# Hybrid streaming step on one core: the recurrence's cross-block scores from one packed product, and the attention value products in groups of four steps

## The reference, cut to what matters

```python
def stick_breaking_block(q, k, v, q_pos, k_pos):
    z = einsum('bthd,bshd->bhts', q, k) * (SB_HEAD_DIM ** -0.5)
    mask = k_pos[None, :] < q_pos[:, None]
    log_fail = where(mask, log_sigmoid(-z), 0.0)
    after = cumsum(log_fail, axis=3, reverse=True) - log_fail
    a = where(mask, exp(log_sigmoid(z) + after), 0.0)
    return einsum('bhts,bshd->bthd', a, v)

def step(S, blk):                      # HGRN2, blocks of time, S: key x value state
    b = cumsum(lfb, axis=1)            # lfb: log of the forget gate
    kb = -expm1(lfb)
    q_dec, k_inv = qb * exp(b), kb * exp(-b)
    att = where(tril, einsum('bthc,bshc->bhts', q_dec, k_inv), 0.0)
    o = einsum('bhts,bshv->bthv', att, vb) + einsum('bthc,bhcv->bthv', q_dec, S)
    k_end = kb * exp(b_end - b)
    S_new = exp(b_end[:, 0])[..., None] * S + einsum('bshc,bshv->bhcv', k_end, vb)
    return S_new, o
```

## Time and profile before

| | |
|---|---|
| timed runs | 1099.53, 1097.09, 1099.34 us; median 1099.34 |
| profiled execution | 1096.95 us, span 1095.2 us, mean granted clock 0.996 |
| PE busy | 1069.7 us, 98% of the span |
| DVE, ACT, POOL busy | 651.4, 571.3, 133.8 us |
| one pair (attention and recurrence stage) | about 163.4 us, four of them |

### The profile page before, as it was taken

The page is one execution under the profiler, slowest core; times in us unless marked ns, Lnnn a source line. Parts: engine busy times, 40 slices in busy tenths (PEclk is TensorE's granted clock), DMA queues, the critical chain, the costliest instruction groups (busy, mean ns, idle before and its releaser), DMA issues.

```text
span 1095.2 us, 16749 instructions
## 1 busy us (share of the span) xinstructions
PE 1069.7 (98%) x6324; PEld 981.6 (90%) x6324; DVE 651.4 (59%) x1143; ACT 571.3 (52%) x1264; POOL 133.8 (12%) x145
## 2 busy tenths in 40 slices
PE   8999999999999999999999999999999999999995
PEld 5998779998779998779998779999999999999994
DVE  6677798387797377797377797345412221362117
ACT  5557883367883467883467884444032223252221
POOL 0001112011012011012011012001200100121220
PEclk9999999999999999999999999999999999999998
DMA  8041031132031132041131130143111111111144
GB/s 294 1 142 37 20 128 49 54 97 91 20 134 43 61 102 79 23 136 39 60 113 69 32 135 29 39 154 136 43 39 40 39 39 58 40 40 39 40 192 172
DMA packets 41487, 84.86 MB, mean 77 GB/s; under 512 B 2112, under 2 KB 22208, under 8 KB 41280
## 3 DMA queue, kind: packets, MB, share of 16 engines
q1 hardware_dynamic: 40832, 81.43, 22.3%
q10 hardware_dynamic: 576, 2.36, 0.6%
HBM read 67.27 MB, written 16.52 MB: 77 GB/s over the span
## 4 chain that ended last, share of the span: by engine, by line
PE 78%; ACT 9%; DVE 9%; issue 3%; DMA 1%; ACTq 0%; POOL 0%; DVEq 0%; SPq 0%; POOLq 0%
PE bank L673 50%; PE bank L1017 9%; DVE E L1682 3%; PE bank L810 3%; ACT E L1303 2%; ACT SPH L1315 2%; PE bank L840 2%; ACT E L1298 2%; DVE E L1686 1%; PE bank L796 1%; PE bank L683 1%; PE bank L710 1%; PE bank L914 1%; PE bank L959 1%; PE bank L981 1%
## 5 line engine op out<-in xcount | busy, mean ns | idle before, releaser
L673 PE MATMUL bank<-xh,wh 128*128 128x384 f32 x1296 | 438.8, 339 | 3.1 <-issue 2.9
L673 PE MATMUL bank<-xh,wl 128*128 128x384 f32 x1296 | 439.8, 339 | 0.0
L673 PE MATMUL bank<-xl,wh 128*128 128x384 f32 x1296 | 439.3, 339 | 0.0
L673 PEld LDWEIGHTS bank<-xh,wh 128*128 128x128 f32 x1296 | 243.5, 188 | 11.1 <-issue 9.3
L673 PEld LDWEIGHTS bank<-xh,wl 128*128 128x128 f32 x1296 | 243.6, 188 | 4.5 <-issue 2.0
L673 PEld LDWEIGHTS bank<-xl,wh 128*128 128x128 f32 x1296 | 243.5, 188 | 3.1 <-issue 0.2
L1188 ACT ACTIVATE slot<-bank,ngate 128x384 f32<-128x384 f32 x48 | 27.7, 578 | 178.0 <-PE bank L673 175.3
L1455 DVE CAST wh<-wr 128x1024 fp32r<-128x1024 f32 x64 | 43.7, 683 | 99.2 <-PE bank L673 98.1
L1460 DVE TENSOR_TENSOR wl<-wr,wh 128x1024 fp32r<-128x1024 f32 x64 | 90.8, 1419 | 1.9
L1682 DVE SCALAR_TENSOR_TENSOR E<-E,bank 128x512 f32<-128x512 f32 (+3 forms) x96 | 53.1, 553 | 47.8 <-ACT E L1303 47.6
L1315 ACT ACTIVATE SPH<-E 128x512 fp32r<-128x512 f32 (+2 forms) x80 | 45.4, 567 | 48.6 <-DVE E L1686 35.3
(11 more groups left out here) (229 smaller groups left out, 1672.8 us busy)
## 6 DMA issues: line engine op xcount, KB each, us to landing
wr<-wch SPq DMA_DIRECT2D x64, 512.0 KB, 3.6
KTc<-ckT SPq DMA_DIRECT2D x4, 2048.0 KB, 9.4
Vc<-cv SPq DMA_DIRECT2D x4, 2048.0 KB, 8.4
graw<-gated SPq DMA_DIRECT2D x8, 576.0 KB, 8.8
xres<-xT SPq DMA_DIRECT2D x1, 4608.0 KB, 14.2
yT<-yb SPq DMA_DIRECT2D x6, 576.0 KB, 3.0
xw<-xT SPq DMA_DIRECT2D x4, 768.0 KB, 11.4
okT<-kT ACTq DMA_DIRECT2D x4, 576.0 KB, 3.0
```

Source lines behind the costliest of these rows:

```text
L673: i = nc.tensor.matmul(CH[n % 2][:, 0:WIN], weights[:, k, :], rows[:, k, w * WIN:(w + 1) * WIN], start=(m == 0), stop=(m == 23))
```

## The change

Recurrence: the operands are packed. `KP` holds per chunk four blocks of keys: blocks 0 and 1 scaled to the middle of the chunk, block 2 scaled to its end, block 0 scaled to its end. `QP` holds per chunk the queries of blocks 2 and 3 (from the middle), of block 3 and of block 1 (from their block's start). One product of 128 weight columns against 128 columns gives all three pieces that ACT copies; they lie at other places of the bank. DVE makes the operands in another order, two scalings now after the wait for the cached attention's tiles (whose space `KP` uses), and a memset goes.

Attention: `Aw` has five buffers. The value products stand in iterations 6, 10, 14, 18, 22 and 26, four steps each (n-6 to n-3), instead of two steps in each even iteration from 4 to 26. To make room the four rows `zr` share two tiles, at partitions 0 and 32, and the high and low row of `RT` change places from tile to tile.

```diff
-        zr = [take(f"zr{i}", [P, QW])[0] for i in range(4)]
-        aw_o = off[0] + 4 * QW
-        Aw = [take(f"Aw{i}", [P, QW])[0] for i in range(3)]
+        zrows = [take(f"zrows{i}", [P, QW])[0] for i in range(2)]
+        aw_o = off[0] + 3 * 4 * QW
+        Aw = [take(f"Aw{i}", [P, QW])[0] for i in range(5)]
...
-        KB = place("KB", [P, HB + 2 * BLK])
-        QB = place("QB", [P, HB])
-        Q1 = place("Q1", [P, HB])
+        KP = place("KP", [P, SEQ])
+        QP = place("QP", [P, SEQ])
...
+        def row_at(n):
+            return 32 * (n % 4 // 2)
+
+        def zr(n, cols):
+            return zrows[n % 2][row_at(n):row_at(n) + 1, cols]
+
+        def row_high(n, cols):
+            return RT[STEPS[n][2]][row_at(n):row_at(n) + 1, cols]
+
+        def row_low(n, cols):
+            return RT[STEPS[n][2]][32 - row_at(n):33 - row_at(n), cols]
...
-                    if n >= 4 and n % 2 == 0:
-                        wd, j, _ = STEPS[n - 4]
-                        c0 = first_col(n - 4)
-                        if n == 4:
+                    if n >= 6 and n % 4 == 2:
+
+                        if n == 6:
                             need(pe, s_oc, 3 * p)
                             pe.wait_ge(s_te, 6 * p + 3)
-                        if j == 4 * wd + 3:
-                            need(pe, s_gA, 2 * p + wd)
                         pe.wait_ge(s_a, NS * p + n - 2)
                         if diagonal(n - 3):
                             pe.wait_ge(s_am, DIAGS * p + diagonals_until(n - 3))
-                        for h in range(2):
-                            r = slice(DH * h, DH * h + DH)
-                            nc.tensor.matmul(OB[r, c0:QW], v_nat[:, j * P + DH * h:j * P + DH * h + DH],
-                                             Aw[(n - 4 + h) % 3][:, c0:QW], start=(j == 4 * wd + 3), stop=(j == 0),
-                                             skip_group_check=True).then_inc(s_av, 1)
+                        for m in range(n - 6, n - 2):
+                            wd, j, h = STEPS[m]
+                            c0, r = first_col(m), slice(DH * h, DH * h + DH)
+                            if j == 4 * wd + 3 and h == 0:
+                                need(pe, s_gA, 2 * p + wd)
+                            nc.tensor.matmul(OB[r, c0:QW], v_nat[:, j * P + DH * h:j * P + DH * h + DH], Aw[m % 5][:, c0:QW],
+                                             start=(j == 4 * wd + 3), stop=(j == 0), skip_group_check=True).then_inc(s_av, 1)
...
                             if c < NCH:
-                                h0 = 2 * BLK * c
-                                nc.tensor.matmul(Z[2][:, P:P + 64], lf[:, cols], Q1[:, h0:h0 + 64], start=True, stop=True)
-                                i = nc.tensor.matmul(Z[2][:, P + 64:2 * P], KB[:, h0:h0 + P], QB[:, h0:h0 + 64],
-                                                     start=True, stop=True)
+                                i = nc.tensor.matmul(Z[2][:, P:2 * P], KP[:, cols], QP[:, cols], start=True, stop=True)
                             i.then_inc(s_at, 1)
...
-                        need(act, s_av, t - 2)
-                        if m < 2:
+                        need(act, s_av, t - 4)
+                        if m < 5:
                             need(act, s_hg, 3 * p)
-                        nc.scalar.activation(Aw[m % 3][:, c0:QW], ZB[m % 4][:, c0:QW], ACT.Exp).then_inc(s_a, 1)
+                        nc.scalar.activation(Aw[m % 5][:, c0:QW], ZB[m % 4][:, c0:QW], ACT.Exp).then_inc(s_a, 1)
...
-                                nc.scalar.activation(a[0:32, 32:64], z[0:32, P:P + 32], ACT.Copy)
-                                nc.scalar.activation(a[64:96, 96:128], z[64:96, P + 32:P + 64], ACT.Copy)
-                                nc.scalar.activation(a[0:64, 64:128], z[0:64, P + 64:2 * P], ACT.Copy).then_inc(s_ato, 1)
+                                nc.scalar.activation(a[0:32, 32:64], z[96:128, P + 96:P + 128], ACT.Copy)
+                                nc.scalar.activation(a[64:96, 96:128], z[64:96, P + 64:P + 96], ACT.Copy)
+                                nc.scalar.activation(a[0:64, 64:128], z[0:64, P:P + 64], ACT.Copy).then_inc(s_ato, 1)
...
-                for r in (0, 2):
-                    i = V.tensor_tensor(blocks(lf)[:, :, r, :], k[:, :, r, :],
...
-                scale(lambda r: blocks(KB, 2)[:, :, r, :], lambda r: k[:, :, r, :], F_HK, 4, 0, 2)
-                V.memset(KB[:, HB:], 0.0).then_inc(s_hke, 1)
+                for r, at in ((2, 2), (0, 3)):
+                    i = V.tensor_tensor(blocks(KP)[:, :, at, :], k[:, :, r, :],
...
+                scale(lambda r: blocks(KP)[:, :, r, :], lambda r: k[:, :, r, :], F_HK, 4, 0, 2).then_inc(s_hke, 1)
```

More of the change, by code:

```diff
@@ L49 @@
 NCH = SEQ // P
-HB = NCH * 2 * BLK
 F_END, F_HK, F_HQ, F_K, F_Q, F_ALL, F_START, F_W = 0, 40, 72, 104, 120, 136, 144, 160
@@ L1300, in _ @@
                             need(act, s_Sl, SUMS * p + (sums_until(n - 4) if n >= 4 else 0))
-                            nc.scalar.activation(zr[n % 4][0:1, row_col(n):QW], ZB[n % 4][0:1, row_col(n):QW], ACT.Copy)
+                            nc.scalar.activation(zr(n, slice(row_col(n), QW)), ZB[n % 4][0:1, row_col(n):QW], ACT.Copy)
                         act.wait_ge(s_E, t + 1)
@@ L1319, in _ @@
                         act.wait_ge(s_S, SUMS * p + sums_until(m))
-                        nc.scalar.activation(RT[STEPS[m][2]][0:1, cols], zr[m % 4][0:1, cols], ACT.Copy).then_inc(s_Sh, 1)
+                        nc.scalar.activation(row_high(m, cols), zr(m, cols), ACT.Copy).then_inc(s_Sh, 1)
                     recurrence_aside(p, n)
@@ L1519, in later_row @@
                 cols = slice(row_col(m), QW)
-                row = zr[m % 4][0:1, cols]
+                row = zr(m, cols)
                 dve.wait_ge(s_a, NS * p + m + 1)
@@ L1524, in later_row_low @@
             def later_row_low(p, m):
-                h, cols = STEPS[m][2], slice(row_col(m), QW)
+                cols = slice(row_col(m), QW)
                 dve.wait_ge(s_Sh, SUMS * p + sums_until(m))
-                V.tensor_tensor(RT[h][32:33, cols], zr[m % 4][0:1, cols], RT[h][0:1, cols].bitcast(F32),
-                                ALU.subtract).then_inc(s_Sl, 1)
+                V.tensor_tensor(row_low(m, cols), zr(m, cols), row_high(m, cols).bitcast(F32), ALU.subtract).then_inc(s_Sl, 1)
             def values_low(p):
@@ L1588, in chunk_operands @@
                 dve.wait_ge(s_as, 2 * (p + 1))
-                scale(lambda r: blocks(KB, 2)[:, :, r, :], lambda r: k[:, :, r, :], F_HK, 4, 0, 2)
-                V.memset(KB[:, HB:], 0.0).then_inc(s_hke, 1)
+                for r, at in ((2, 2), (0, 3)):
+                    i = V.tensor_tensor(blocks(KP)[:, :, at, :], k[:, :, r, :],
+                                        fac[:, F_END:F_END + NBLK].rearrange("c (n r) -> c n r", r=4)[:, :, r, None].broadcast_to([P, NCH, BLK]),
+                                        ALU.mult)
+                i.then_inc(s_hke, 1)
+                scale(lambda r: blocks(KP)[:, :, r, :], lambda r: k[:, :, r, :], F_HK, 4, 0, 2).then_inc(s_hke, 1)
                 dve.wait_ge(s_hqd, p + 1)
                 for r in range(2):
-                    i = V.tensor_tensor(blocks(Q1, 2)[:, :, r, :], q[:, :, 2 * r + 1, :],
+                    i = V.tensor_tensor(blocks(QP)[:, :, 3 - r, :], q[:, :, 2 * r + 1, :],
                                         fac[:, F_START:F_W].rearrange("c (n r) -> c n r", r=2)[:, :, r, None].broadcast_to([P, NCH, BLK]),
@@ L1596, in chunk_operands @@
                 i.then_inc(s_hke, 1)
-                scale(lambda r: blocks(QB, 2)[:, :, r - 2, :], lambda r: q[:, :, r, :], F_HQ, 4, 2, 4).then_inc(s_hke, 1)
+                scale(lambda r: blocks(QP)[:, :, r - 2, :], lambda r: q[:, :, r, :], F_HQ, 4, 2, 4).then_inc(s_hke, 1)
                 scale(lambda r: blocks(QA)[:, :, r, :], lambda r: q[:, :, r, :], F_HQ, 4, 0, 2)
@@ L1941, in _ @@
                         pool.wait_ge(s_a, NS * p + m + 1)
-                        G.tensor_tensor(Aw[m % 3][:, c0:c0 + P], Aw[m % 3][:, c0:c0 + P], causal, ALU.mult).then_inc(s_am, 1)
+                        G.tensor_tensor(Aw[m % 5][:, c0:c0 + P], Aw[m % 5][:, c0:c0 + P], causal, ALU.mult).then_inc(s_am, 1)
                     for w12 in ended(B_PIECES[n]):
```

3 lines of the change are left out of this document (removed).

## The result

The change made the kernel slower. The runs of after have a median of 1109.74 us (1109.23 to 1110.74), those of before beside them 1098.33 us (1097.09 to 1099.53); the ratio is 1.0105, 95% interval [1.0088, 1.0123]. The forecast was 1092.3 us, range 1085.0 to 1096.5, so it missed the sign as well. The cause is the edit that I had priced at nothing: the rows at partition 32. Of all executions one stands apart, one of before in the last group of runs, with 3698.71 us; without it that group's median is 1097.92 us instead of 1098.07.

What follows compares the result with a forecast made beforehand. PE was taken to bound the recurrence stage and the ACT-DVE loop most of the attention stage. 1096.95 - 7.0 (scores) - 0 (value products) = 1089.9 us profiled, so a median of 1092.3 us, range 1085.0 to 1096.5.

Steps and rivals of the forecast that it cites:

- The recurrence scores: Recurrence stage: one packed product replaces two, saving 0.22 us a chunk, 7.0 us in all.
- The value products as PE's work: Attention stage: joining groups of value products saves PE about 0.36 us a join, 8.6 us of work in all.
- rival C: Attention groups of four: the two heads no longer run side by side, ending at 1104 to 1109 us; chance 0.05.
- PE's waits for the rows: Attention stage: PE's waits go up by some 2 us a pair as its saved work turns into waiting.
- The value products as time: Attention stages: PE's saving is worth 0 as time, between 8.6 us gained and 4.0 us lost.
- the exp of step 11: Attention stage, iteration 10: the bigger group delays ACT's exp from 268.44 to 268.80, losing 0.36 us.
- Rival A: Whole kernel: PE sets the pace everywhere, 15.6 us gained, median 1083.7; chance 0.27 with the mixed cases.
- the joins: Attention value products: 6 joins of two groups a pair, 24 in all, about 0.36 us of PE work each.
- The rows at partition 32: Attention stage: rows moved to partition 32 cost what they cost at partition 0, so nothing was counted.
- the loop of ACT and DVE: Attention stage: the round trip ACT, DVE, ACT bounds most of it, with PE keeping just in step.

Runs made afterwards that it cites:

- e1: Kernel before with the packed recurrence scores alone: 1090.83 us, ratio 0.9942.
- e7: Changed kernel with all rows at partition 0, two streams' keys loaded late but ahead of the values: 1094.04 us, ratio 0.9969.
- e11: e7 with the copy of the row's high part moved from ACT to DVE: 1085.13 us, ratio 0.9878.
- e2: Kernel before with its four rows in two tiles at partitions 0 and 32, nothing else: 1111.73 us, ratio 1.0134.
- e8: Kernel before with all four rows and their high parts at partition 32, in four tiles: 1126.69 us, ratio 1.027.
- e10: e1 with the copy of the row's high part moved from ACT to DVE: 1080.9 us, ratio 0.9849.
- e14: e11 with the first copy of the row moved to DVE as well: 1105.78 us, ratio 1.007.
- e12: e8 with the high part of the row back at partition 0: 1121.58 us, ratio 1.0213.
- e3: Changed kernel with all rows at partition 0, two streams' keys loaded late, behind the values: 1111.04 us, ratio 1.0128.

## Why the prediction was wrong

**The recurrence scores: right.** Forecast 0.22 us a chunk, 1.75 a pair, 7.0 in all. Measured 0.22 in the chunk, 1.54 a pair between the marks, 6.4 in e1 by the medians; seven of the eight chunks give it, the last one with what follows it up to the next pair's first score gives nothing. The formula for the issue gap in the Trainium skill ("TensorE: Matmul & The Clock Gate", Back-to-back issue gap), by which only the streamed columns count and this edit gives nothing, doesn't hold for these fp32 products. The same section says that in a real kernel the matmul and the load of its weights both set the spacing. The trace agrees with that part, with 0.21 to 0.22 us at 16 as at 128 columns.

**The value products as PE's work: right.** A group of 384 and 512 columns takes 1.66 us (1.65 forecast), and the two heads run side by side, so rival C's mechanism is out. PE's waits for the rows are 12.1 us in e7 and 4.1 in e1, the 2 us a pair more that were forecast. The drain at a mode switch, of which the Trainium skill speaks ("TensorEngine Tiling (Array Packing)", Key Properties), agrees with the trace: the joined group of iteration 10 costs 0.36 us beyond its columns (272.27 - 270.13 = 2.14, less 0.17, 0.12 and 1.49 for 896 columns), which is what each of the two groups had cost alone. That it comes off as time is what the runs deny. That the outcome lies just above C's 1104 to 1109 us is chance; its cause was another.

**The value products as time: 0 forecast, 0.8 us a pair measured by the medians of e7 and e1 (0.7 between the marks), 3.2 in all**, inside the bounds (8.6 gained to 4.0 lost). Two terms are to be seen. At iteration 10 I expected the exp of step 11 to be held up by 0.36 us. In e7 the two exps are

```profile
264.12 0.39 ACT L1307 ACTIVATE E<-bank 128x256 f32<-128x256 f32 x1 [0.57 <-PE bank L823]
...
267.84 0.39 ACT L1307 ACTIVATE E<-bank 128x256 f32<-128x256 f32 x1 [0.60 <-PE bank L823]
```

3.72 us apart, against 268.44 - 265.35 = 3.09 before: held up by 0.63. The 0.27 us more than expected are a reading that I had wrong. I took it that ACT may read the scores 0.55 us after their start. From scores to exp it is 0.83 us before (267.61 to 268.44), since this exp waits for the sums' product behind them as well (L810, 267.95 to 268.34), and 0.82 in e7. ACT had hardly any slack there. The 0.6 us are won back late, behind the weights of step 22: first score to last `Aw` is 84.73 in both kernels in this pair, 0.16 longer on average over four. The other term I had left out. Behind the last `Aw` nothing is left for PE but filler and value products. In e1 two of these products stand there, in e7 four:

```profile
319.87 0.57 ACT L1320 ACTIVATE Aw<-bank 128x512 f32<-128x512 f32 x1
322.23 1.94 PE L853 MATMUL bank<-Aw,v_nat 128*64 128x512 f32 x8
```

The start of the last `Aw` to the end of the stage is 3.71 us in e1 and 4.23 in e7, 0.5 more, since 0.85 us of columns moved behind the last weights and one join saves 0.36 of it. Rival A fell with the same numbers, and by e11 the joins would not have come off as time with ACT relieved either.

**The rows at partition 32: the step that failed.** "The rows at partition 32 cost what they cost at partition 0, one row each, as far as any row tells." They cost 14.5 us alone (e2) and 14.6 in the change (after against e7, each against the before of its own runs). This term stood in the sum as nothing, without a row; the rest of the change, with the rows at partition 0 (e7), measures 1094.04 us, 1.7 above the forecast and inside the range.

The trace of before had no row for it, and here I broke my own rule: an operation that the trace doesn't show is bounded from both sides. ACT's order of time in before would have given a bound. ACT's instructions overlap by some 0.10 us (exp and copy 0.11, copy and logarithm 0.10); if two copies lose that on both sides, it is 0.4 us a step, times 8 steps and 4 pairs 13 us. The runs make it 0.5 us a step, because an instruction that doesn't overlap starts 0.01 to 0.03 us after the end: 0.13 + 0.12 around the first copy, 0.11 + 0.14 around the second (`SPH` at 254.16 to the exp at 255.15 in after against 251.04 to 251.78 in before). That is 16 us, of which 14.5 show. In the rows of 512 columns, 16 of the 32 at partition 32, the loss ahead of the second copy is DVE's, as said at e8; an estimate from its 0.12 us is 2 us of the 16. And that the loop of ACT and DVE is the bound, which the prediction had read rightly, means that nearly all of these tenths count.

**The sum.** Packed scores -6.4 (e1), groups +3.2 (e7 against e1), rows +14.5 (e2, measured alone): 11.3 us. Measured 1109.74 - 1098.33 = 11.4 in the runs beside each other.

## What to carry to other kernels

When an edit moves an operand to another partition, count it as an edit, even if shape and count stay: look at the distance between the starts of the instructions around it, on every engine that touches it, since the durations hardly change. An engine whose busy time grows with the same instructions may have lost overlap. When a loop between two engines is the bound, look for the short instruction that fits into the other engine's wait (e10), and leave alone the one that would stand ahead of that engine's next due result (e14); and before joining work into bigger groups look at what then stands behind the last input.

## What the runs showed of the hardware

- ACT's neighbours overlap by 0.09 to 0.11 us, at 256, 384 and 512 columns. The overlap is lost, 0.11 to 0.14 us in all, when an instruction writes at another partition (0 or 32) than its predecessor wrote, or reads at another one than the last reader of the same memory (table at e12).
- DVE loses overlap in the same place: from mask to row 0.36 us with the row at 0 and 0.50 at 32 (256 columns), from clamp to row 0.61 and 0.72 (512 columns).
- After PE had stood still for 3.1 us in e3, the granted clock was 0.54 from 335 to 337 us, 1.3 us after PE had gone on, and 1.00 before.
- Copies of one row of 256 columns last 0.36 or 0.37 us in either place.
- The same cast of one row of 256 columns takes 0.28 us on DVE in e10, and the next DVE instruction starts 0.21 after it:

```profile
241.46 0.28 DVE L1517 CAST RT<-zr 1x256 fp32r<-1x256 f32 x1
241.67 0.41 DVE L1688 TENSOR_TENSOR SPL<-E,SPH 128x256 fp32r<-128x256 f32 x1
```

On ACT it took 0.42 us, with 0.33 to the next. The moved instruction was also the cheaper one.
